# Loading and turning the memory rows tile by tile behind their own norm vector, with the other norm vectors, the x rows and the angle tables placed later

## The chip, the cores and the metric

The kernel runs on one core of one Trainium2 chip. The metric is the device time of one launch in microseconds. A launch has an execution span (from the first to the last instruction of the core) and about 2 us around it.

## What is computed

A two block transformer layer with 256 tokens (two tiles of 128 rows) of width 1024, in float32, each block with a memory of 256 rows. The change touches only what opens the first block: the keys and values of the memory branch, and the norm of the tokens.

```python
def rms_norm(x, g):
    xf = x.astype(jnp.float32)
    y = xf * lax.rsqrt(jnp.mean(xf * xf, axis=-1, keepdims=True) + EPS)
    return (y * g.astype(jnp.float32)).astype(x.dtype)
...
        h = rms_norm(x, g_norm[layer])
        proj = h @ w_in[layer]
...
        kv_m = (rms_norm(mem, g_mem[layer]) @ w_mem_kv[layer]).reshape(b, m_len, 2, M_HEADS, M_HEAD_DIM)
        k_m = rms_norm(kv_m[:, :, 0], g_kn_m[layer])
        v_m = kv_m[:, :, 1]
```

After that come three attention branches with gates, a second block (differential attention, a gated linear recurrence, cross attention), and a mixture of 32 experts of which each token takes two. The cosine and sine tables of the positions are needed when the queries and keys of the first block are rotated.

## The kernel before, in words

Each engine has its own program, written by hand in the order in which it runs; semaphores join them. There is no scheduler, so the order of the code is the order of the work.

The opening, engine by engine. SyncE issues the loads: all 256 memory rows in one transfer (1 MB, into R1v), the first weight block "mk" (columns 0 to 511 of w_mem_kv: row blocks 0 and 1, row blocks 2 and 3, then row blocks 4 to 7), the token rows x (1 MB, into X3), the second weight block "mv" (2 MB), then "cq" and "small". The weight blocks turn through three slots of a ring, so "small" waits until the product of "mk" is done, and "qi" until that of "mv" is. ScalarE issues nine small loads of norm vectors into the 55 rows of GR (g_norm first, g_mem second) and the positions.

TensorE turns (transposes) the 55 rows of norm vectors at once, then the memory rows (four groups of four 128 by 128 transposes, into four banks of PSUM), runs `project("mk", ...)` (two token tiles, eight row blocks i each, 16 matmuls), turns the x rows, and runs `project_blocks("mv", ...)`: seven half-size products m0 to m6 that take the place of eight. m2 and m3 take sums of weights (S_a, S_b), m4 and m6 take the changed blocks w21 and w12; GpSimd makes these four in `weight_sums` (16 additions, each of 128 by 256), and counts them in w_sums. m2 to m5 take sums of the turned rows, which VectorE makes in `row_sums`. m4 is the first product that writes to the accumulator that "mk" used, so it waits until ScalarE has emptied it.

In the profile each float32 matmul or transpose of 128 rows stands as two records.

VectorE copies the turned norm vectors to GC, multiplies the turned memory rows by g_mem while moving them out of PSUM (`drain_rows`), computes the reciprocal root for the memory rows (12 small instructions in `rsqrt`), waits for the squares of x, scales x (`norm_rows`), makes the row sums of memory, makes the arguments of the angle tables (16 small instructions), drains the turned x rows, and combines the products of "mv" (`combine`). The tokens' squares are taken by ScalarE only after VectorE has given the scale of the memory rows (mem_scaled). ScalarE's sine (L1507) waits for the arguments (trig_arg), and its emptying of "mk" (`drain_mem`, L1512) is behind the sine in its program.

After "mv" the order on TensorE is "cq", "small", "qi" and so on; before "cq" it waits until the x rows are drained.

Of the kernel before, what the change touches and what calls it, by code (L numbers as in the profile page):

```python
# [20 lines left out]
ALU = mybir.AluOpType  # L21
ACT = mybir.ActivationFunctionType
AX_X = mybir.AxisListType.X

P = 128
D = 1024
# [26 lines left out]
GC_NORM, GC_MEM, GC_MIX, GC_CROSS, GC_MEM2, GC_CQ, GC_CKV, GC_GATEB, GC_FFN, GC_N = 0, 8, 16, 24, 32, 40, 43, 45, 47, 55  # L53
# [3 lines left out]
def two_block_layer(nc, A, out):  # L57
    ctx = ExitStack()
    with ctx:
# [3 lines left out]
        def sem(name):  # L63
            return ctx.enter_context(nc.semaphore(name))
# [149 lines left out]
        mem_landed = sem("mem_landed")  # L214
# [231 lines left out]
        for t in range(TT):  # L446
# [5 lines left out]
            ("g_norm", GC_NORM, 8), ("g_mem", GC_MEM, 8), ("norm_mix_2", GC_MIX, 8), ("norm_cross_2", GC_CROSS, 8),  # L452
# [41 lines left out]
        def _(pe):  # L494
# [8 lines left out]
            def aux(b, key):  # L503
                n = aux_uses[b]
                aux_uses[b] += 1
                aux_no[key] = (b, n)
                if n:
                    pe.wait_ge(aux_free[b], n)
                return AUX[b], aux_full[b]
# [229 lines left out]
            pe.wait_ge(consts_ready, 1)  # L739
            pe.wait_ge(gains_landed, 16 * len(gains))  # L740
            bank, full = aux(3, "gains")
            nc.tensor.transpose(bank[:, 0:GC_N], GR[:, :], ident[0:GC_N, 0:GC_N]).then_inc(full, 1)
            pe.wait_ge(mem_landed, 16)
            for t in range(TT):
                for g in range(2):
                    turn(2 * t + g, ("mem", t, g))
            project("mk", R2T)
            turn_rows("x0", 0)
            project_blocks("mv", R2T, T_x, mem_sums)
# [441 lines left out]
        def _(sp):  # L1191
            sp.dma_start(R1v, rows(A["mem"])).then_inc(mem_landed, 16)
            for c, (name, width, parts) in enumerate(chunks):
                if slot_before[c]:
                    wait_full(sp, last_job[slot_before[c]])
                for first, src in parts:
                    k, n = src.shape[1], src.shape[2]
                    dst = slot_of(name)[:, 0:k, first:first + n]
                    if c == 0:
                        for i in range(2):  # L1200
                            sp.dma_start(dst[:, 2 * i:2 * i + 2, :], src[:, 2 * i:2 * i + 2, :]).then_inc(first_landed[i], 16)
                        dst, src = dst[:, 4:KD, :], src[:, 4:KD, :]
                    sp.dma_start(dst, src).then_inc(slot_landed[slot_no[c]], 16)
# [75 lines left out]
        def _(pool):  # L1279
# [8 lines left out]
            g.memset(ident[:, :], 0.0)  # L1288
# [7 lines left out]
            for j in range(16):  # L1296
# [3 lines left out]
            g.affine_select(out=ident[:, :], in_=ident[:, :], compare_op=ALU.not_equal, fill=1.0, base=0,  # L1300
                            pattern=[[-1, P]], channel_multiplier=1)
# [126 lines left out]
        def _(act):  # L1428
# [69 lines left out]
            for dst, src in gains:  # L1498
                act.dma_start(dst, src).then_inc(gains_landed, 16)
# [3 lines left out]
            square_rows(0, R1v, R3v, [(mem_landed, 16)])  # L1503
            act.wait_ge(mem_scaled, 1)
            square_rows(1, X3, ZTv, [(x_landed, 16)])
            act.wait_ge(trig_arg, 2)
            a_.activation(trig[:, 128:192], trig[:, 64:128], ACT.Sin).then_inc(trig_ready, 1)  # L1507
# [14 lines left out]
            last.then_inc(mv_scaled, 1)  # L1522
            drain("cq", by_token(PJ3, PJ_CQ, 384))
# [231 lines left out]
        def _(dve):  # L1755
# [198 lines left out]
            bank = wait_full(dve, "gains")  # L1954
            v.tensor_copy(GC[:, :], bank[:, 0:GC_N]).then_inc(free_sem("gains"), 1)
            wait_drained(dve, "gains")
            drain_rows("mem", R2T, GC_MEM)
# [3 lines left out]
            norm_rows(1, X3, ZTv, 2)  # L1961
            row_sums(T_x, quarters(R2T), mem_sums)

# [18 lines left out]
            drain_rows("x0", XT3, GC_NORM)  # L1982
            combine("mv", by_rows(R1v, 512))
# [459 lines left out]
```

## Time and profile before

| | |
|---|---|
| median of three runs | 1104.6 us (1104.5 to 1105.12) |
| the profiled execution's own time | 1104.28 us |
| its span | 1102.5 us |
| busy in the span | TensorE 921.5 us, VectorE 405.2 us, GpSimd 244.4 us, ScalarE 166.9 us |
| first matmul record | 9.17 us after the span's start |
| start of "cq" | 42.85 us |
| moved between 720 and 1080 us | 427 GB/s all the time |

The shares are means over stages with different limits. The last 420 us stream the experts' weights, and the DMA engines are the ones that are full there; before that TensorE is busy nearly all the time, except in the opening, where it has nothing to do for 9 us.

### The profile page before, as it was taken

Reading aid. Unit: us, or ns where it says so; the run is one execution under the profiler, and the core shown is the slowest. Engines: PE = TensorE matmul, PEld = TensorE weight load, DVE = VectorE, ACT = ScalarE, POOL = GpSimd, SP = SyncE. Lnnn points to the kernel's source line nnn. Section 1 sums busy time; section 2 is a strip of 40 time slices with the busy share of each in tenths; the row PEclk is TensorE's granted clock in tenths of the full one; section 3 lists DMA queues with packets and bytes.
Section 4 is the critical chain, followed back from the end, with each engine's and each line's share of the span. In section 5 each row is a group of like instructions: output and inputs, shape, how many; then the busy total and the mean of one; then the engine's idle time right before and its main releaser. Section 6 shows DMA issues by size and latency. Waiting matters only on the chain.

```text
span 1102.5 us, 12492 instructions
## 1 busy us (share of the span) xinstructions
PE 921.5 (84%) x5006; PEld 569.7 (52%) x5006; DVE 405.2 (37%) x994; ACT 166.9 (15%) x372; POOL 244.4 (22%) x366
## 2 busy tenths in 40 slices
PE   6999999999999999999999998757465566473757
PEld 3774487889999878864445653222222122131312
DVE  4736836663223746868445433010101001010101
ACT  2113223441001013013302230000000000000000
POOL 4442143044654958930000000000000000000000
PEclk9999999999999999999999999878878878687879
DMA  7645342232445344524419649999999999999996
GB/s 286 168 146 191 121 153 78 77 130 100 157 168 207 105 171 169 201 87 153 153 68 346 252 173 428 427 429 427 428 428 427 427 428 427 428 429 427 427 416 272
DMA packets 64328, 290.38 MB, mean 263 GB/s; under 512 B 9031, under 2 KB 11918, under 8 KB 51726
## 3 DMA queue, kind: packets, MB, share of 16 engines
q1 hardware_dynamic: 57840, 205.13, 48.6%
q10 hardware_dynamic: 6430, 84.44, 18.1%
q8 instruction: 41, 0.67, 0.3%
q14 instruction: 17, 0.14, 0.0%
HBM read 288.51 MB, written 1.05 MB: 263 GB/s over the span
## 4 chain that ended last, share of the span: by engine, by line
PE 62%; DMA 26%; DVE 6%; issue 2%; another core or an unknown queue 2%; ACT 2%; ACTq 0%; SPq 0%; DVEq 0%
DMA ring<-in_w_e_up_dram 12%; PE ACC L535 10%; PE ACC L691 10%; DMA BIG<-in_w_e_up_dram 9%; PE ACC L550 9%; PE PAIR L1086 8%; PE ACC L688 7%; PE ACC L574 5%; DMA PJ<-in_w_e_up_dram 4%; PE ACC L977 3%; PE PAIR L585 2%; PE PAIR L1117 2%; PE PAIR L662 1%; PE PAIR L639 1%
## 5 line engine op out<-in xcount | busy, mean ns | idle before, releaser
L1337 POOL TENSOR_TENSOR ring<-ring 128x256 f32<-128x256 f32 x272 | 205.3, 785 | 167.3 <-PE ACC L688 75.5
L1086 PE MATMUL PAIR<-ring,R 128*32 128x512 f32 x400 | 130.4, 708 | 41.2 <-DMA BIG<-in_w_e_up_dram 20.8
L550 PE MATMUL ACC<-BIG,ring 128*128 128x256 f32 (+1 forms) x464 | 103.8, 381 | 0.6 <-DVE R L1921 0.6
L550 PEld LDWEIGHTS ACC<-BIG,ring 128*128 128x128 f32 (+1 forms) x464 | 85.4, 187 | 15.5 <-issue 3.1
L2378 DVE SCALAR_TENSOR_TENSOR GB<-GB,PAIR 128x512 f32<-128x512 f32 x8 | 5.5, 688 | 231.8 <-ACT GB L1728 231.8
L1086 PE MATMUL PAIR<-BIG,R 128*32 128x512 f32 x176 | 62.8, 727 | 22.1 <-DMA PJ<-in_w_e_up_dram 22.1
L1086 PE MATMUL PAIR<-R 128*32 128x512 f32 x176 | 59.7, 695 | 25.0 <-DMA ring<-in_w_e_up_dram 12.5
L1117 PE MATMUL PAIR<-ring,BIG 128*32 128x512 f32 x160 | 64.5, 747 | 18.0 <-DMA R<-in_w_e_down_dram 12.4
L535 PE MATMUL ACC<-ring,BIG 128*128 128x512 f32 (+2 forms) x192 | 78.1, 559 | 0.5 <-DVE R L2214 0.5
L1086 PE MATMUL PAIR<-SQE,R 128*32 128x512 f32 x112 | 61.4, 711 | 17.0 <-DMA ring<-in_w_e_up_dram 10.7
L1086 PEld LDWEIGHTS PAIR<-ring,R 128*32 128x32 f32 x400 | 30.9, 128 | 73.2 <-issue 73.2
L691 PE MATMUL ACC<-ring 128*128 128x256 f32 x288 | 64.9, 381 | 1.9 <-ACT R L1512 1.0
L535 PE MATMUL ACC<-ring,R 128*128 128x512 f32 (+1 forms) x136 | 59.1, 584 | 0.7 <-DVE R L2007 0.4
L691 PEld LDWEIGHTS ACC<-ring 128*128 128x128 f32 x288 | 54.3, 190 | 10.4 <-issue 1.8
L1117 PE MATMUL PAIR<-PJ,BIG 128*32 128x512 f32 x128 | 46.7, 746 | 14.4 <-DMA ring<-in_w_e_down_dram 14.4
L2380 DVE SCALAR_TENSOR_TENSOR GB<-GB,PAIR 128x512 f32<-128x512 f32 x8 | 8.4, 1052 | 131.8 <-PE PAIR L1086 131.8
L574 PE MATMUL ACC<-ring,BIG 128*128 128x512 f32 x128 | 55.8, 592 | 0.0
L1086 PE MATMUL PAIR<-PJ,R 128*32 128x512 f32 x160 | 50.8, 698 | 5.7 <-DMA ring<-in_w_e_up_dram 5.0
L535 PEld LDWEIGHTS ACC<-ring,BIG 128*128 128x128 f32 x192 | 35.6, 190 | 35.2 <-issue 27.0
L688 PE MATMUL ACC<-ring 128*128 128x128 f32 x384 | 45.1, 276 | 0.0
L688 PEld LDWEIGHTS ACC<-ring 128*128 128x128 f32 x384 | 44.1, 192 | 0.7 <-issue 0.5
L691 PE MATMUL ACC<-ring,R 128*128 128x256 f32 x184 | 40.9, 379 | 0.0
(346 smaller groups left out, 1402.5 us busy)
## 6 DMA issues: line engine op xcount, KB each, us to landing
ring<-in_w_in_dram SPq DMA_DIRECT2D x20, 2048.0 KB, 7.9
ring<-in_w_e_gate_dram SPq DMA_DIRECT2D x8, 2048.0 KB, 40.1
ring<-in_w_e_up_dram SPq DMA_DIRECT2D x6, 2048.0 KB, 41.1
ring<-in_w_e_gate_dram ACTq DMA_DIRECT2D x6, 2048.0 KB, 26.5
ring<-in_w_e_down_dram SPq DMA_DIRECT2D x5, 2048.0 KB, 39.1
ring<-in_w_e_up_dram ACTq DMA_DIRECT2D x5, 2048.0 KB, 20.9
ring<-in_w_ckv_dram SPq DMA_DIRECT2D x4, 2048.0 KB, 8.0
BIG<-in_w_e_down_dram SPq DMA_DIRECT2D x4, 2048.0 KB, 22.9
```

Source lines behind the costliest of these rows:

```text
L535: mm = nc.tensor.matmul(bank[:, t * 512:t * 512 + width], lhs[:, i, t * P:(t + 1) * P], w[:, i, a:a + width], start=(i == 0), stop=(i == k ...
L550: mm = nc.tensor.matmul(bank[0:m, j * S:(j + 1) * S], w[:, i, a + j * P:a + j * P + m], rhs[:, i, :], start=(i == 0), stop=(i == k - 1))
L574: mm = nc.tensor.matmul(bank[:, c:c + 512], lhs[:, i, t * P:(t + 1) * P], w[:, i, :], start=(i == order[0]), stop=(i == order[-1]))
L585: mm = nc.tensor.transpose(bank[0:src.shape[1], j * P:(j + 1) * P], src, ident[:, :])
L639: mm = nc.tensor.transpose(bank[:, (j * heads + i) * P:(j * heads + i + 1) * P], e[:, i, j * P:(j + 1) * P], ident[:, :])
L662: mm = nc.tensor.matmul(bank[:, d * 256:(d + 1) * 256], value(j, h, d), p[:, j * 256:(j + 1) * 256], start=first, stop=last)
L688: mm = nc.tensor.matmul(bank[:, j * P:(j + 1) * P], left[:, k, j * P:(j + 1) * P], right[:, k, :], start=(k == 0), stop=(k == 3))
L691: mm = nc.tensor.matmul(bank, right[:, k, :], left[:, k, :], start=(k == 0), stop=(k == 3))
L977: mm = nc.tensor.matmul(ACC[t][:, h * 512:(h + 1) * 512], XT3[:, i, t * P:(t + 1) * P], slot_of(f"wco{h}")[:, i, :], start=False, stop=Fal ...
L1086: mm = nc.tensor.matmul(bank[r, :], M_xt[:, k, r], w[e][:, k, :], start=(k == 0), stop=(k == KD - 1))
L1117: mm = nc.tensor.matmul(AUX[2 + h][r, :], M_hidt[:, k, r], w[e][:, k, h * 512:(h + 1) * 512], start=(k == 0), stop=(k == 3))
L1337: ins = g.tensor_tensor(out[:, k, :], a[:, k, :], b[:, k, :], op)
```

## The change

The load of the memory rows is split into its two tiles; the second is issued behind row blocks 0 to 3 of "mk". The norm vector g_mem moves to the front of GR and of ScalarE's loads and gets a semaphore of its own; it is turned alone, and the other vectors are turned later, inside "mk", together with the second tile of memory rows. GpSimd finishes the identity matrix first and signals it. The turning of x moves from ahead of "mv" to behind its fourth product. On VectorE the row sums of memory move ahead of the norm of x, the angle arguments behind the combination of "mv"; on ScalarE the squares of x move ahead of the wait for mem_scaled, and the sine behind the emptying of "mk" and "mv".

```diff
-GC_NORM, GC_MEM, GC_MIX, ... = 0, 8, 16, ...
+GC_MEM, GC_NORM, GC_MIX, ... = 0, 8, 16, ...
...
 TensorE
-            pe.wait_ge(consts_ready, 1)
-            pe.wait_ge(gains_landed, 16 * len(gains))
-            bank, full = aux(3, "gains")
-            nc.tensor.transpose(bank[:, 0:GC_N], GR[:, :], ident[0:GC_N, 0:GC_N]).then_inc(full, 1)
-            pe.wait_ge(mem_landed, 16)
-            for t in range(TT):
+            pe.wait_ge(ident_ready, 1)
+            pe.wait_ge(mem_gain_landed, 16)
+            nc.tensor.transpose(ACC[1][:, 0:8], GR[0:8, :], ident[0:8, 0:8]).then_inc(mem_gain_turned, 1)
+
+            def turn_mem(t):
+                pe.wait_ge(mem_landed[t], 16)
                 for g in range(2):
                     turn(2 * t + g, ("mem", t, g))
-            project("mk", R2T)
-            turn_rows("x0", 0)
-            project_blocks("mv", R2T, T_x, mem_sums)
+            def turn_rest(done, total):
+                if done == 4:
+                    turn_mem(1)
+                    pe.wait_ge(gains_landed, 16 * (len(gains) - 1))
+                    nc.tensor.transpose(ACC[1][:, 512:512 + GC_N], GR[:, :], ident[0:GC_N, 0:GC_N]).then_inc(gains_turned, 1)
+
+            turn_mem(0)
+            pe.wait_ge(consts_ready, 1)
+            project("mk", R2T, after=turn_rest)
+            pe.wait_ge(gains_ready, 2)
+            project_blocks("mv", R2T, T_x, mem_sums, after=lambda done: turn_rows("x0", 0) if done == 16 else None)
...
 SyncE
-            sp.dma_start(R1v, rows(A["mem"])).then_inc(mem_landed, 16)
+            sp.dma_start(R1v[:, 0, :], A["mem"][0, 0:P, :]).then_inc(mem_landed[0], 16)
...
                             sp.dma_start(dst[:, 2 * i:2 * i + 2, :], src[:, 2 * i:2 * i + 2, :]).then_inc(first_landed[i], 16)
+                        sp.dma_start(R1v[:, 1, :], A["mem"][0, P:2 * P, :]).then_inc(mem_landed[1], 16)
...
 GpSimd
-            g.memset(ident[:, :], 0.0)
+            link(g.memset(ident[:, :], 0.0))
+            g.affine_select(out=ident[:, :], in_=ident[:, :], compare_op=ALU.not_equal, fill=1.0, base=0,
+                            pattern=[[-1, P]], channel_multiplier=1).then_inc(ident_ready, 1)
...
 ScalarE
-            for dst, src in gains:
+            act.dma_start(*gains[0]).then_inc(mem_gain_landed, 16)
+            for dst, src in gains[1:]:
                 act.dma_start(dst, src).then_inc(gains_landed, 16)
...
-            square_rows(0, R1v, R3v, [(mem_landed, 16)])
+            act.wait_ge(mem_landed[0], 16)
+            a_.activation(R3v[:, 0, :], R1v[:, 0, :], ACT.Square, scale=D ** -0.5, accum_out=SMALL[:, 64:65])
+            square_rows(0, R1v, R3v, [(mem_landed[1], 16)], [1])
+            square_rows(1, X3, ZTv, [(x_landed, 16)], col=66)
             act.wait_ge(mem_scaled, 1)
-            square_rows(1, X3, ZTv, [(x_landed, 16)])
-            act.wait_ge(trig_arg, 2)
-            a_.activation(trig[:, 128:192], trig[:, 64:128], ACT.Sin).then_inc(trig_ready, 1)
...
             last.then_inc(mv_scaled, 1)
+            act.wait_ge(trig_arg, 2)
+            a_.activation(trig[:, 128:192], trig[:, 64:128], ACT.Sin).then_inc(trig_ready, 1)
             drain("cq", by_token(PJ3, PJ_CQ, 384))
...
 VectorE
-            bank = wait_full(dve, "gains")
-            v.tensor_copy(GC[:, :], bank[:, 0:GC_N]).then_inc(free_sem("gains"), 1)
-            wait_drained(dve, "gains")
-            drain_rows("mem", R2T, GC_MEM)
+            dve.wait_ge(mem_gain_turned, 1)
+            v.tensor_copy(GC[:, 0:8], ACC[1][:, 0:8]).then_inc(gains_ready, 1)
+            dve.wait_ge(gains_ready, 1)
+            drain_rows("mem", R2T, GC_MEM, [0])
+            drain_rows("mem", R2T, GC_MEM, [1])
+            dve.wait_ge(gains_turned, 1)
+            v.tensor_copy(GC[:, 8:GC_N], ACC[1][:, 520:512 + GC_N]).then_inc(gains_ready, 1)
+            dve.wait_ge(gains_ready, 2)
             dve.wait_ge(rows_squared, 1)
             rsqrt(2, SMALL[:, 64:66])
             v.tensor_copy(SMALL[:, 74:76], RS[:, 0:2]).then_inc(mem_scaled, 1)
-            norm_rows(1, X3, ZTv, 2)
+            for t in range(TT):
+                for g in range(2):
+                    wait_drained(dve, ("mem", t, g))
             row_sums(T_x, quarters(R2T), mem_sums)
+            norm_rows(1, X3, ZTv, 2, col=66)
+            drain_rows("x0", XT3, GC_NORM)
+            combine("mv", by_rows(R1v, 512))
...
-            drain_rows("x0", XT3, GC_NORM)
-            combine("mv", by_rows(R1v, 512))
             dve.wait_ge(small_landed, small_total)
```

TensorE's program at its start, before (PAIR and ACC are banks of PSUM, SQE holds the norm vectors, R the memory rows and later their turned form, BIG the x rows and later their turned form, ring the weights; one row for each instruction, xN for N alike):

```order
L742 MATMUL PAIR<-ident,SQE 128x55
L585 MATMUL PAIR<-ident,R 128x128 x16
L535 MATMUL ACC<-ring,R 128x512 x16
L585 MATMUL PAIR<-ident,BIG 128x128 x16
L691 MATMUL ACC<-ring,R 128x256 x8
L691 MATMUL ACC<-ring 128x256 x16
L691 MATMUL ACC<-ring,R 128x256 x4
L535 MATMUL ACC<-ring,BIG 128x384 x16
```

The same place in the changed kernel (its line numbers are a few higher):

```order
L745 MATMUL ACC<-ident,SQE 128x8
L589 MATMUL PAIR<-ident,R 128x128 x8
L539 MATMUL ACC<-ring,R 128x512 x4
L589 MATMUL PAIR<-ident,R 128x128 x8
L756 MATMUL ACC<-ident,SQE 128x55
L539 MATMUL ACC<-ring,R 128x512 x12
L695 MATMUL ACC<-ring,R 128x256 x8
L695 MATMUL ACC<-ring 128x256 x8
L589 MATMUL PAIR<-ident,BIG 128x128 x16
L695 MATMUL ACC<-ring 128x256 x8
L695 MATMUL ACC<-ring,R 128x256 x4
L539 MATMUL ACC<-ring,BIG 128x384 x16
```

Half of the memory's transposes moved into "mk" behind its fourth matmul, with the turning of all vectors behind them; the x transposes moved from ahead of "mv" to between its fourth and fifth products.

ScalarE's program behind its loads, before (the table load at L1507 and the activation with PJ are the sine):

```order
L1442 ACT_TABLE_LOAD
L1442 ACTIVATE BIG,SMALL<-R 128x1024 x2
L1442 ACTIVATE BIG,SMALL<-BIG 128x1024 x2
L1507 ACT_TABLE_LOAD
L1507 ACTIVATE PJ<-PJ 128x64
L1512 ACTIVATE R<-ACC,SMALL 128x512 x2
L1452 ACTIVATE SQE<-R 128x1024
L1521 ACTIVATE R<-R,SMALL 128x512 x2
L1458 ACTIVATE PJ<-ACC 128x384 x2
```

The same place in the changed kernel:

```order
L1519 ACT_TABLE_LOAD
L1519 ACTIVATE BIG,SMALL<-R 128x1024
L1456 ACTIVATE BIG,SMALL<-R 128x1024
L1456 ACTIVATE BIG,SMALL<-BIG 128x1024 x2
L1527 ACTIVATE R<-ACC,SMALL 128x512 x2
L1466 ACTIVATE SQE<-R 128x1024
L1536 ACTIVATE R<-R,SMALL 128x512 x2
L1539 ACT_TABLE_LOAD
L1539 ACTIVATE PJ<-PJ 128x64
L1472 ACTIVATE PJ<-ACC 128x384 x2
```

The sine and its table load moved from ahead of the emptying of "mk" (R<-ACC) to behind the scaling of "mv", just ahead of the emptying of "cq".

## Rows read from the trace of the kernel before

**Rows 1.** The page: busy time, share of the span, instructions.

```profile
PE 921.5 (84%) x5006; PEld 569.7 (52%) x5006; DVE 405.2 (37%) x994; ACT 166.9 (15%) x372; POOL 244.4 (22%) x366
```

**Rows 2.** The chain that ended last, 0 to 120 us: start, us, what.

```profile
4.21 4.82 DMA SQE<-in_norm_ffn_dram
...
36.36 1.16 ACT R L1512 x2
```

**Rows 3.** Timeline of TensorE: start, us, what, idle before with releaser.

```profile
9.42 3.67 PE L585 MATMUL PAIR<-ident,R 128*128 128x128 f32 x16
12.89 15.02 PE L535 MATMUL ACC<-ring,R 128*128 128x512 f32 x32
27.75 1.91 PE L585 MATMUL PAIR<-ident,BIG 128*128 128x128 f32 x16
...
37.56 3.72 PE L691 MATMUL ACC<-ring 128*128 128x256 f32 x16 [1.00 <-ACT R L1512]
...
42.85 20.16 PE L535 MATMUL ACC<-ring,BIG 128*128 128x384 f32 x64
```

**Rows 4.** DMA issues, 0 to 60 us: size, median us to landing; then SyncE's first issue.

```profile
R<-in_mem_dram SPq DMA_DIRECT2D x1, 1024.0 KB, 5.0
ring<-in_w_mem_kv_dram SPq DMA_DIRECT2D x2, 512.0 KB, 6.7
ring<-in_w_mem_kv_dram SPq DMA_DIRECT2D x1, 1024.0 KB, 9.8
...
0.82 0.44 SPq L1192 DMA_DIRECT2D R<-in_mem_dram  x1
2.39 0.65 SPq L1203 DMA_DIRECT2D ring<-in_w_mem_kv_dram  x1
```

**Rows 5.** DMA queue of ScalarE, 0 to 2 and 2.5 to 3 us (packets); all queues, 4.5 to 5.

```profile
q10 hardware_dynamic: 12, 0.00, 0.6%
q10 hardware_dynamic: 4, 0.00, 0.8%
4.50:5.00 0.50, 0.00 (x0) 0.00 (x0) 0.00 (x0) 0.00 (x0) 0.23 (x2) 1.00 1.02 401
```

**Rows 6.** Timeline of GpSimd.

```profile
4.64 0.15 POOL L1312 MEMSET MASKS<- 64x64 f32 x1
20.30 10.93 POOL L1337 TENSOR_TENSOR ring<-ring 128x256 f32<-128x256 f32 x12 [15.51 <-DMA ring<-in_w_mem_kv_dram]
33.26 2.77 POOL L1337 TENSOR_TENSOR ring<-ring 128x256 f32<-128x256 f32 x4 [2.03 <-PE ACC L691]
```

**Rows 7.** Matmuls of "mk", 12.8 to 13.3 and 15.6 to 16.2 us: busy, mean ns.

```profile
L535 PE MATMUL ACC<-ring,R 128*128 128x512 f32 x1 | 1.1, 1061 | 0.0
L535 PE MATMUL ACC<-ring,R 128*128 128x512 f32 x3 | 1.5, 592 | 0.0
```

**Rows 8.** Timeline of VectorE.

```profile
22.43 2.31 DVE L1793 TENSOR_SCALAR BIG<-BIG,RS 128x1024 f32<-128x1024 f32 x2
24.67 1.21 DVE L1935 TENSOR_TENSOR ring<-R 128x512 f32<-128x512 f32 x1
...
35.42 0.65 DVE L1979 TENSOR_SCALAR PJ<-PJ 128x32 f32<-128x32 f32 x1
36.10 2.48 DVE L1806 TENSOR_TENSOR BIG<-PAIR,GC 128x512 f32<-128x512 f32 x4
...
39.74 0.42 DVE L1917 TENSOR_TENSOR R<-ACC,R 128x256 f32<-128x256 f32 x1
...
65.91 0.17 DVE L1767 TENSOR_SCALAR NW<-SMALL 128x4 f32<-128x4 f32 x1 [11.38 <-ACT SQE L1531]
```

**Rows 9.** Timeline of ScalarE.

```profile
53.37 0.87 ACT L1458 ACTIVATE PJ<-ACC 128x384 f32<-128x384 f32 x2 [8.53 <-PE ACC L535]
```

**Rows 10.** SyncE's waits, 560 to 700 us; then the window of the expert stage.

```profile
SPq L1245 <- PE ACC L977: 29.8, 2, 20.6
720.00:1080.00 360.00, 220.89 (x1480) 81.88 (x1484) 29.74 (x64) 13.04 (x24) 0.00 (x0) 0.79 1.01 427
```

More of the change, by code:

```diff
@@ L51 @@
 PJ_QA, PJ_KA, PJ_VA, PJ_QI, PJ_KI, PJ_WI, PJ_CKV, PJ_KR, PJ_CQ, PJ_QM, PJ_W = 0, 512, 1024, 1536, 2048, 2112, 2120, 2376, 2408, 2792, 3304
-GC_NORM, GC_MEM, GC_MIX, GC_CROSS, GC_MEM2, GC_CQ, GC_CKV, GC_GATEB, GC_FFN, GC_N = 0, 8, 16, 24, 32, 40, 43, 45, 47, 55
+GC_MEM, GC_NORM, GC_MIX, GC_CROSS, GC_MEM2, GC_CQ, GC_CKV, GC_GATEB, GC_FFN, GC_N = 0, 8, 16, 24, 32, 40, 43, 45, 47, 55
 GB_A, GB_B, GB_M, GB_DA, GB_DAO, GB_GLAO, GB_X, GB_ROUTE, GB_LAM, GB_N = 0, 128, 320, 576, 704, 832, 960, 1472, 1508, 1764
@@ L213, in two_block_layer @@
         x_landed = sem("x_landed")
-        mem_landed = sem("mem_landed")
+        mem_landed = [sem(f"mem_landed{t}") for t in range(TT)]
+        mem_gain_landed = sem("mem_gain_landed")
+        mem_gain_turned = sem("mem_gain_turned")
+        gains_turned = sem("gains_turned")
+        ident_ready = sem("ident_ready")
         mem2_landed = sem("mem2_landed")
@@ L451, in two_block_layer @@
         gains = [(GR[r:r + n, :], A[name][0].rearrange("(k p) -> k p", p=P)) for name, r, n in (
-            ("g_norm", GC_NORM, 8), ("g_mem", GC_MEM, 8), ("norm_mix_2", GC_MIX, 8), ("norm_cross_2", GC_CROSS, 8),
+            ("g_mem", GC_MEM, 8), ("g_norm", GC_NORM, 8), ("norm_mix_2", GC_MIX, 8), ("norm_cross_2", GC_CROSS, 8),
             ("norm_mem_2", GC_MEM2, 8), ("g_cq", GC_CQ, 3), ("g_ckv", GC_CKV, 2),
@@ L1299, in _ @@
             g.tensor_copy(iota[:, :], iota_i[:, :])
-            g.affine_select(out=ident[:, :], in_=ident[:, :], compare_op=ALU.not_equal, fill=1.0, base=0,
-                            pattern=[[-1, P]], channel_multiplier=1)
             g.affine_select(out=causal[:, 128:256], in_=causal[:, 128:256], compare_op=ALU.is_ge, fill=NEG, base=0,
```

## The prediction

> **What bounds the kernel now.** I read the shares of busy time first [rows 1]: TensorE is busy for 84% of the span, no other engine for half of it. Then the chain that ended last [rows 2]. It opens with the last norm vector, whose load is issued at 4.21 and takes 4.82 us to land, and later it runs over ScalarE's emptying of "mk" at 36.36. The timeline of TensorE [rows 3] shows both as idle time: its first transposes of memory rows start only at 9.42, and ahead of 37.56 stands a wait of 1.00 us for ScalarE. Between these, and up to the start of "cq" at 42.85, it has no other gap. So two things bound the opening: what TensorE waits for before its first work, and that one wait. The expert stage at the end is bound otherwise: from 720 to 1080 us 427 GB/s are moved without a break, with TensorE busy 221 of 360 us [rows 10]. A gain in the opening reaches the end only if that stream starts earlier too. Its first loads are issued when TensorE has finished something (SyncE waits 29.8 us for the matmuls of L977 in two waits) [rows 10], so it should move along.
>
> **The start.** The changed kernel needs for its first memory transposes: the first memory tile, g_mem turned, and the identity. The 1 MB of memory rows is issued at 0.82 and lands 5.0 us later, at 5.8 [rows 4]; half of it is 0.52 MB less, which at 401 GB/s is 1.3 us [rows 5]. So the first tile lands at about 4.5. g_mem is now the first load on ScalarE's queue. In the trace the first one is g_norm, with eight rows: 12 packets of that queue ran before 2 us and 4 between 2.5 and 3 [rows 5], which is eight rows and eight counts, so I take 3.0 for it. GpSimd's last constant ends at 4.79 [rows 6]; the identity is now its first. So the memory transposes start at 4.5 in place of 9.42: **4.9 us**. As bounds I take 4.2 us (the half tile saves only half of the 1.3 us) and 5.5 us: GpSimd's constants at 4.79, a copy (0.2 us) and a drain (0.69 us) let no first matmul start before 5.7, and the forecast has 6.3.
>
> **"mk".** 16 transposes take 3.5 us (9.42 to 12.89), so the first eight end at 6.2. VectorE may not begin before its constants (4.8), then drains a group in 0.69 us at most (four took 2.48 [rows 8]), so the first matmul starts at about 6.3. Row blocks 0 to 3 of "mk" lie in two loads of 512 KB. With the first memory tile ahead they are the second and third half megabyte, at about 5.8 and 7.1; in time. Here the clock matters. The granted clock in the profile's rows is 1.00 for all of the opening, but the records speak otherwise: the first matmul of "mk" has 1061 ns, those after 15.6 have 592 ns [rows 7]. The transposes too run at 0.22 us each at 9.42 and at 0.12 us at 27.75 [rows 3]. So until about 15.4 (between the two rows), 6.0 us after its first transpose, the engine ran at 1.2 GHz, then at 2.4. I let the slow stretch keep its 6.0 us: 4.5 to 10.5. Then "mk" has done 4.2 us of slow work by 10.5, which is 2.1 us at full speed; four matmuls are 3.4 us at full speed (a quarter of 15.02 less the 1.3 lost between 12.89 and 15.4), so they end at 11.8. The second memory tile landed at about 8.5; eight transposes (1.0 us) and the turned vectors (0.1) end at 12.9. The last half of "mk" weights lands at 2.39 + 9.8 = 12.2 [rows 4]; no wait. The other 12 matmuls take 10.3 us: "mk" ends at 23.2, against 27.75. Of the 4.9 us 4.6 are still there; the gain work and handing over cost 0.3.
>
> **"mv".** GpSimd starts on the sums at 20.30, when the weights land, and the bytes ahead of them stay the same [rows 6]. They are 12 additions in 10.93 us and 4 in 2.77: 23.9, 27.6, 31.2 and 34.1 are the ends of the four sums at the rate of before, if it no longer waits 2.03 us for TensorE in between. TensorE now reaches m0 at 23.2, each product takes 1.8 us (two in 3.72 [rows 3]): m2 at 26.8, m3 at 28.6, the x transposes 30.4 to 32.3, m4 at 32.3, m5 at 34.1, m6 at 35.9, end 37.7. Each lies behind its sum, by 2.9, 1.0, 1.1 and 1.8 us. The x transposes, which stood ahead of "mv", cover GpSimd's third sum. The wait of 1.00 us goes, since ScalarE empties "mk" at 23.3 with no sine ahead: **1.0 us**. By differences: the seven products and the x transposes took 43.0 - 27.75 = 15.2 us, less 1.0 is 14.2, and 23.2 + 14.2 = 37.4. I take 37.4, a gain of **5.6 us** at the start of "cq".
>
> **VectorE.** The x rows must be scaled by 30.4. Memory is drained at 13.6, then a root of 12 small instructions (2.4 us), row sums (4.6 us at most, from four of 1.1 to 1.2 [rows 8]), another root, and the scaling (2.31 us for two tiles). Beside GpSimd's additions a small instruction takes 0.65 us, otherwise 0.17 [rows 8]. That gives 26 us as I expect it, and with every instruction slow 30.4 for the first tile: no wait, or one of some tenths. The drains of x (2.5 us) end at 33; the combination's third part (three instructions of 0.42 us [rows 8]) follows m5 and frees the bank for "cq" at 37.2. Cover: 0.2 us only, so what is late here next is this bank.
>
> **What moved behind.** The angle arguments took 6.9 us (29.2 to 36.1 [rows 8]) and now start at 37.8. They are beside four additions of GpSimd, as before; 7 us, 45. The sine is needed by ScalarE before it empties "cq", which is full at 37.4 + 10.1 = 47.5 (it was at 53.37 [rows 9]). Then the memory keys' norm (7 us) to 52, and the next thing on VectorE, the latents' root, is due at 65.91 - 5.6 = 60.3 [rows 8]; it idled 11.38 us ahead of it before. So these moves cost nothing. The extra load instruction on SyncE (0.44 us) is covered by the full DMA queue.
>
> **Sum.** 4.9 + 1.0 - 0.3 = 5.6 us off an execution of 1104.28 (span 1102.5): 1098.7. The median is 0.3 above this execution, so 1099.0.
>
> **A rule against the change.** The loads of the opening follow each other at 401 GB/s with 512 KB pieces among them [rows 5], so one more piece costs nothing that I can see. The Trainium skill, page SBUF — State Buffer, section on the DMA setup-cost knee, says that each transfer pays about 2 us that don't scale with bytes and that one should coalesce into the largest transfer; by that the last half of "mk" would land 2 us later, and the sum would be about 3.5 in place of 5.6. The trace disagrees as far as it shows queued loads.
>
> **The rivals.**
> - *The slow clock lasts longer or shorter.* Work is now thinner at the start, with a drain to wait for. If the clock rises when the fourth matmul is done instead of at 10.5, these end at 6.3 + 6.8 = 13.1 and not 11.8: 1.3 us lost, and the eight transposes half a us more, 1100.8. If it rises as long after the first matmul as before (15.4 - 12.9 = 2.5, at 8.8), the four end at 11.0, but the weights at 12.2 stop the gain at 0.7: 1098.3. The Trainium skill (TensorE: Matmul & The Clock Gate, what's actually happening) calls the number of slow matmuls at a start run-variable.
> - *A load lands later than worked out.* Cutting the memory load moves later ones by a us or two: "mk" waits at its fifth matmul from 12.9 to 14.2, and the sums of "mv" shift too. 1.3 to 2.1 us lost: 1100.3 to 1101.1. For it: the fifth matmul comes only 0.7 us behind its weights now. Against it: no byte is added ahead of "mk".
> - *The gain does not reach the end.* The expert stream is full for 400 us; if its start hung on a load and not on TensorE, the end would stay: 1104.6. Against it stand SyncE's waits [rows 10].
> - *Slower: VectorE's queue.* Angle arguments and the keys' norm stand ahead of the latents' root in one queue. If both ran three times as long beside GpSimd (0.65 for 0.17 us on each small instruction and more), 14 us would be 42, ending at 80 instead of 60.3. It decides from 28 us on: 22.5 us is the cover, and 5.6 more eat the gain. In the trace the arguments already ran half of their time beside GpSimd and took 6.9 us, so I see no such thing; 1105 to 1110 if it came.
>
> **How the numbers follow.** The forecast (1098.4 to 1100.0) has 0.57, the clock earlier 0.10, clock later 0.12, loads later 0.11, no gain at the end 0.06, slower 0.04. The range 1097.9 to 1101.4 holds the first four. Within 0.2% (2.2 us, about what a measurement of this kernel can tell from no change) is only a gain lost almost wholly. Faster 0.91, same 0.05, slower 0.04.
>
> **What would show it.** First memory transpose at 4.5; records of 1061 ns until about 10.5; no idle TensorE ahead of the fifth matmul of "mk", of m3, m4 and m6; ScalarE's emptying of "mk" right behind its end; "cq" from 37.3. From there on every start should be 5.6 earlier up to the last store. It is wrong if the first transposes start after 6, if GpSimd's sums end after 36, or if the stream between 680 and 1080 does not move.

## The result

The changed kernel takes 1098.42 us (1098.32 to 1098.58, four runs) against 1104.55 us (1103.96 to 1105.12, four runs) of the kernel before: ratio 0.9945, 95% interval 0.9933 to 0.9957. It is 6.1 us faster; 5.6 was forecast. The profiled execution took 1098.47 us, with a span of 1096.6.

The page after, busy time by engine, hardly differs from before [rows 1]:

```profile
PE 922.8 (84%) x5007; PEld 569.3 (52%) x5007; DVE 403.1 (37%) x995; ACT 167.2 (15%) x372; POOL 243.1 (22%) x366
```

Timeline of TensorE of the changed kernel (start, us, line, what; in brackets the idle time ahead with its releaser), which answers to [rows 3]:

```profile
3.15 0.24 PE L745 MATMUL ACC<-ident,SQE 8*128 8x8 f32 x1 [3.15 <-DMA SQE<-in_g_mem_dram]
4.66 1.97 PE L589 MATMUL PAIR<-ident,R 128*128 128x128 f32 x8 [1.27 <-DMA R<-in_mem_dram]
6.68 4.68 PE L539 MATMUL ACC<-ring,R 128*128 128x512 f32 x8
11.20 1.04 PE L589 MATMUL PAIR<-ident,R 128*128 128x128 f32 x8
...
12.51 10.54 PE L539 MATMUL ACC<-ring,R 128*128 128x512 f32 x24
22.89 3.62 PE L695 MATMUL ACC<-ring,R 128*128 128x256 f32 x16
...
29.80 1.91 PE L589 MATMUL PAIR<-ident,BIG 128*128 128x128 f32 x16
31.54 3.62 PE L695 MATMUL ACC<-ring 128*128 128x256 f32 x16
...
36.73 20.16 PE L539 MATMUL ACC<-ring,BIG 128*128 128x384 f32 x64
```

The memory transposes start at 4.66 in place of 9.42, the end of "mk" is at 22.89 in place of 27.75, and "cq" starts at 36.73 in place of 42.85. So 4.86 us are there at the end of "mk", and the rest of the 6.12 us, 1.26, comes inside "mv", where the wait for ScalarE ahead of m4 is gone.

The chain that ended last, in the changed kernel's first 60 us (start, us, what). The vectors' load, VectorE and ScalarE, which it ran over before [rows 2], are no longer in it:

```profile
0.82 3.80 DMA R<-in_mem_dram
...
4.66 1.97 PE PAIR L589 x8
...
12.51 10.54 PE ACC L539 x24
...
31.71 5.18 PE ACC L695 x24
```

Timelines of GpSimd, VectorE and ScalarE in the changed kernel, which answer to [rows 6, 8, 9]:

```profile
20.52 12.24 POOL L1351 TENSOR_TENSOR ring<-ring 128x256 f32<-128x256 f32 x16 [15.50 <-DMA ring<-in_w_mem_kv_dram]
```

```profile
15.82 0.69 DVE L1952 TENSOR_TENSOR ring<-R 128x512 f32<-128x512 f32 x1
...
21.29 2.31 DVE L1810 TENSOR_SCALAR BIG<-BIG,RS 128x1024 f32<-128x1024 f32 x2
30.43 2.48 DVE L1823 TENSOR_TENSOR BIG<-PAIR,GC 128x512 f32<-128x512 f32 x4 [6.83 <-PE PAIR L589]
...
36.00 0.42 DVE L1938 TENSOR_TENSOR R<-ACC,R 128x256 f32<-128x256 f32 x1
...
37.38 0.97 DVE L1993 CAST NW<-pos_i 128x2 f32<-128x2 int32 x1
...
59.79 0.17 DVE L1784 TENSOR_SCALAR NW<-SMALL 128x4 f32<-128x4 f32 x1 [7.87 <-ACT SQE L1548]
```

```profile
23.15 1.27 ACT L1527 ACTIVATE R<-ACC,SMALL 128x512 f32<-128x512 f32 x2 [5.99 <-PE ACC L539]
...
44.68 0.26 ACT L1539 ACTIVATE PJ<-PJ 128x64 f32<-128x64 f32 x1 [4.66 <-DVE PJ L2005]
47.25 0.87 ACT L1472 ACTIVATE PJ<-ACC 128x384 f32<-128x384 f32 x2 [2.31 <-PE ACC L539]
```

The 16 additions run through in 12.24 us without a wait. The row sums of memory run at 15.82, before GpSimd starts, at 0.69 us each; before they stood beside its additions at 1.21. ScalarE empties "mk" at 23.15, as soon as it is full. The sine is at 44.68 and "cq" is there to be emptied at 47.25, after 2.31 us of idle time, so the cover of the sine is 2.3 us. The latents' root still finds VectorE idle for 7.87 us.

The gain reaches the end. SyncE's loads of w_co, before at 572.24, and the late first-round loads of the experts, before at 658.54, have moved by 6.14 and 6.15 us (SyncE's timeline, changed kernel):

```profile
566.10 0.99 SPq L1217 DMA_DIRECT2D ring<-in_w_co_dram  x2
...
652.39 3.33 SPq L1259 DMA_DIRECT2D BIG<-in_w_e_down_dram  x2
```

The stream behind moves 426 GB/s from 720 to 1080 us, 427 before [rows 10]. The store of the result is issued at 1091.27, before at 1097.51; the spans differ by 5.9 us, since the end behind that issue was 0.3 us longer in this profile.

### The profile page after: what moved, and what is told of

It reads as the page before. It is cut to its first block, busy times and chain, and to the rows that moved or that the text cites. A ratio compares the mean times of both kernels' runs of the same rounds, so it can differ in the third digit from the quotient of the medians.

```text
span 1096.6 us, 12500 instructions
## 1 busy us (share of the span) xinstructions
PE 922.8 (84%) x5007; PEld 569.3 (52%) x5007; DVE 403.1 (37%) x995; ACT 167.2 (15%) x372; POOL 243.1 (22%) x366
## 4 chain that ended last, share of the span: by engine, by line
PE 62%; DMA 31%; DVE 5%; ACT 1%; issue 1%; SPq 0%; DVEq 0%; ACTq 0%
DMA ring<-in_w_e_up_dram 12%; PE ACC L539 12%; PE ACC L695 10%; DMA PJ<-in_w_e_up_dram 9%; DMA BIG<-in_w_e_up_dram 9%; PE ACC L554 9%; PE PAIR L1099 7%; PE ACC L692 7%; PE ACC L578 5%; PE ACC L990 3%; PE PAIR L589 2%; PE PAIR L666 1%; PE PAIR L643 1%; PE PAIR L724 1%; PE PAIR L1130 1%
## 5 line engine op out<-in xcount | busy, mean ns | idle before, releaser
L1130 PE MATMUL PAIR<-PJ,BIG 128*32 128x512 f32 x128 | 47.5, 759 | 13.3 <-DMA ring<-in_w_e_down_dram 13.3
```

The costliest lines, as they stand in the source:

```text
L1130: mm = nc.tensor.matmul(AUX[2 + h][r, :], M_hidt[:, k, r], w[e][:, k, h * 512:(h + 1) * 512], start=(k == 0), stop=(k == 3))
```

## The experiments

Single executions of one kernel differed by up to 3.6 us within one group, more than some of the effects, and the medians of the kernel before lie between 1103.99 and 1104.55 us from group to group. So beside each median stands the start of "cq" in the profiled execution: 42.85 before, 36.73 changed. What comes behind it is the same work in all kernels. The start of "cq" too holds a part that is no work of the edit: in the eight profiles without dummy matmuls the first four matmuls of "mk" took between 4.24 and 5.77 us, by when the records get fast.

**One part alone: sine and angle arguments.**

```diff
 kernel before; ScalarE
-            act.wait_ge(trig_arg, 2)
-            a_.activation(trig[:, 128:192], trig[:, 64:128], ACT.Sin).then_inc(trig_ready, 1)
...
             last.then_inc(mv_scaled, 1)
+            act.wait_ge(trig_arg, 2)
+            a_.activation(trig[:, 128:192], trig[:, 64:128], ACT.Sin).then_inc(trig_ready, 1)
 VectorE: drain_rows("x0", ...) and combine("mv", ...) ahead of the angle arguments
```

> The kernel before, with one part of the change alone: the angle arguments on VectorE behind the combination of mv, and the sine on ScalarE behind the scaling of mv. Theory (the gain is an earlier start plus the wait of m4 that goes): m4 no longer waits, 1.0 us of idle time and 0.26 us of refilling go, so 1.2 to 1.3 us off, about 1103.3, with TensorE's first transposes still near 9.4. Rival (the wait only changes hands, because something else than the sine is late, or the other moves are needed for it): 1104.5, with another releaser ahead of m4 or of cq.

Measured: 1102.66 us (before 1104.07; ratio 0.9982, 0.9973 to 0.9992), 1.4 us off. TensorE's timeline:

```profile
9.20 3.67 PE L585 MATMUL PAIR<-ident,R 128*128 128x128 f32 x16
12.67 14.44 PE L535 MATMUL ACC<-ring,R 128*128 128x512 f32 x32
...
32.14 7.07 PE L691 MATMUL ACC<-ring 128*128 128x256 f32 x32
...
40.77 19.56 PE L535 MATMUL ACC<-ring,BIG 128*128 128x384 f32 x62
```

"cq" is 2.08 us earlier than before, of which 0.22 is the start, 0.59 "mk" with fewer slow records (14.44 for 15.02), and the rest, 1.27, the wait: the four products from 32.14 on now run without one. The theory holds, and the wait needs none of the other moves to go. The interval of the times (0.9 to 3.0 us off) fits this and shuts out the rival's nothing.

**The memory in one load.**

```diff
 changed kernel; SyncE
-            sp.dma_start(R1v[:, 0, :], A["mem"][0, 0:P, :]).then_inc(mem_landed[0], 16)
+            sp.dma_start(R1v, rows(A["mem"])).then_inc(mem_landed[0], 16)
...
-                        sp.dma_start(R1v[:, 1, :], A["mem"][0, P:2 * P, :]).then_inc(mem_landed[1], 16)
 TensorE and ScalarE: the waits for the second tile are for this load
```

> The changed kernel with the memory rows in one load of 1 MB at the front, both tiles still turned where the change puts them. Theory (start of TensorE set by the landing of the first memory tile): first transposes at 5.8 to 5.9 in place of 4.66, everything 1.2 us later, about 1099.6. Rival (the fifth matmul of mk waits for its weights at 12.35 whatever comes ahead, so that the split is hidden): 1098.4 to 1098.8.

Measured: 1100.31 us (before 1104.07; ratio 0.9962, 0.9948 to 0.9976).

```profile
5.99 1.97 PE L589 MATMUL PAIR<-ident,R 128*128 128x128 f32 x8 [3.39 <-DMA R<-in_mem_dram]
8.01 4.30 PE L539 MATMUL ACC<-ring,R 128*128 128x512 f32 x8
...
13.30 10.57 PE L539 MATMUL ACC<-ring,R 128*128 128x512 f32 x24
```

The start is 1.33 us later, "cq" at 37.55 only 0.82 later, since the four matmuls took 4.30 instead of 4.68 us and the changed kernel had arrived just at its weights. The profiled execution was the fastest of five (1098.81). By the medians the split is worth 1.9 us against the changed kernel's 1098.42 and 1.0 against its 1099.35 of the last group: about 1 us, and not known more closely. The rival, in which nothing is lost, falls.

**All vectors turned ahead of memory.**

```diff
 changed kernel; TensorE, ahead of the memory rows
-            nc.tensor.transpose(ACC[1][:, 0:8], GR[0:8, :], ident[0:8, 0:8]).then_inc(mem_gain_turned, 1)
+            pe.wait_ge(gains_landed, 16 * (len(gains) - 1))
+            nc.tensor.transpose(ACC[1][:, 0:GC_N], GR[:, :], ident[0:GC_N, 0:GC_N]).then_inc(mem_gain_turned, 1)
 TensorE: no second turning inside "mk"; VectorE: all 55 columns copied at once
```

> The changed kernel, but TensorE waits for all nine norm vectors and turns them at once ahead of the memory rows. Theory: first transposes near 9.3, 4.6 us later than in the changed kernel; only the wait of m4 stays removed, so 1103.0 to 1103.4. Rival (the vectors, now loaded beside a smaller first transfer, land much earlier, since the queue of ScalarE was held up by the 1 MB load): start at 5 to 7 and 1099 to 1101.

Measured: 1102.24 us (1101.4 to 1104.23; ratio 0.998, 0.997 to 0.9989), "cq" at 41.58, 4.85 us later than changed.

```profile
8.92 0.32 PE L746 MATMUL ACC<-ident,SQE 55*128 55x55 f32 x1 [8.92 <-DMA SQE<-in_norm_ffn_dram]
...
11.19 5.55 PE L539 MATMUL ACC<-ring,R 128*128 128x512 f32 x8
```

The memory transposes start at 9.17, 4.51 us later, and the slow records cost 0.87 us more in this execution. It took 1103.57, which is 5.1 more than the profiled execution of the changed kernel; the medians are 3.8 us apart, and 2.9 with the changed kernel's 1099.35. So the vector of its own is the largest part of the gain, 3 to 4 us of time and 4.5 of start. The rival falls: a smaller first transfer does not free ScalarE's queue, the last vector still lands at 8.9.

**The x transposes ahead of "mv".**

```diff
 changed kernel; TensorE
-            project_blocks("mv", R2T, T_x, mem_sums, after=lambda done: turn_rows("x0", 0) if done == 16 else None)
+            turn_rows("x0", 0)
+            project_blocks("mv", R2T, T_x, mem_sums)
```

> The changed kernel with the x transposes ahead of mv again, as before. The prediction had them cover GpSimd's third sum, which it put at 31.2. The trace of the changed kernel has all four sums done at 32.76, so the third near 30, and m4 at 31.54. Theory now: m2 at 28.2, m3 at 30.0, m4 at 31.6 all lie behind their sums, and x is scaled by 23.6; the order is worth nothing or 0.1 to 0.7 us for the wait of the second x tile: 1098.4 to 1099.1. Rival (the cover is needed): a wait at m4 of 1 us or more, 1099.4 and above.

Measured: 1098.8 us (ratio 0.9953, 0.9936 to 0.997), "cq" at 36.71. This move is worth nothing: the cover that the prediction gave the x transposes is not needed. The profile shows no wait at m2 to m6, but one ahead of the fifth matmul of "mk", where TensorE came earlier than its weights this time:

```profile
12.50 10.54 PE L539 MATMUL ACC<-ring,R 128*128 128x512 f32 x24 [0.45 <-DMA ring<-in_w_mem_kv_dram]
```

**Sine and arguments back.** The edit of the first experiment undone in the changed kernel.

```diff
 changed kernel; ScalarE, ahead of drain_mem
+            act.wait_ge(trig_arg, 2)
+            a_.activation(trig[:, 128:192], trig[:, 64:128], ACT.Sin).then_inc(trig_ready, 1)
 VectorE: the angle arguments ahead of drain_rows("x0", ...) and combine("mv", ...)
```

> The changed kernel with the angle arguments on VectorE ahead of the x drains again and the sine ahead of the emptying of mk. Theory: the arguments start at 23.6 beside GpSimd's additions, where a small instruction takes 0.65 us, and end at 31 to 34.5; the sine, the emptying of mk and the x drains follow, so m4 waits 1 to 4 us and cq for the x drains: 1100.5 to 1102.5. Rival (with the earlier start there is room for them): 1098.4 to 1098.9.

Measured: 1105.1 us (1103.4 to 1107.04; ratio 1.0005, 0.9995 to 1.0014): the whole gain is gone, more than I expected (1102.5 at most). TensorE's timeline, and its windows (busy of PE, weight loads, VectorE, ScalarE, GpSimd; granted clock, DMA share, GB/s) of this kernel:

```profile
30.98 1.91 PE L589 MATMUL PAIR<-ident,BIG 128*128 128x128 f32 x16
37.14 6.03 PE L695 MATMUL ACC<-ring 128*128 128x256 f32 x16 [4.25 <-ACT R L1529]
```

```profile
33.00:37.00 4.00, 0.00 (x0) 0.00 (x0) 3.78 (x11) 2.61 (x4) 0.00 (x0) 0.75 0.14 39
37.00:40.00 3.00, 2.86 (x7) 2.33 (x8) 1.34 (x4) 1.14 (x2) 0.00 (x0) 0.50 0.71 115
40.00:42.00 2.00, 2.00 (x7) 1.62 (x6) 0.00 (x0) 0.00 (x0) 0.00 (x0) 0.54 0.23 52
42.00:45.00 3.00, 3.00 (x15) 2.59 (x14) 1.25 (x4) 0.00 (x0) 0.00 (x0) 1.00 0.07 12
```

The wait at m4 is 4.25 us, just above the 4 that I expected at most. VectorE and ScalarE show why (arguments; sine; emptying of "mk"):

```profile
27.12 0.69 DVE L1990 CAST NW<-pos_i 128x2 f32<-128x2 int32 x1
```

```profile
35.68 0.26 ACT L1524 ACTIVATE PJ<-PJ 128x64 f32<-128x64 f32 x1
35.84 1.25 ACT L1529 ACTIVATE R<-ACC,SMALL 128x512 f32<-128x512 f32 x2
```

The arguments start at 27.12 and not at the 23.6 of the forecast, because the root of the x rows ahead of them began 1.3 us later than in the first profile of the changed kernel (19.66 for 18.36) and so fell beside the additions (0.65 us for a small instruction). GpSimd starts these when the weights land, at 20.57, and that did not move. "mk" is emptied from 35.84 on, before from 36.26 in the same view: TensorE started 4.54 us earlier, and 0.42 of it are left at m4. So the two gains do not simply add up. The sine moved alone is worth 1.3 us; without it the earlier start comes back as a longer wait.

During the wait the granted clock fell, at 35.0, to 0.50 of full, and it stayed there until 41.8, so m4 and m5 took 6.03 us and not 3.62. The wait alone is 4.25, the fallen clock 2.4 more. This execution was the slowest of ten (1107.04); the fastest was at 1103.4, and I take it, without a profile of it, that the clock did not fall or not as long there.

**Dummy matmuls, and the weights of "mk" in more parts.** The first kernel adds eight matmuls of the identity by itself, into a bank that "mk" overwrites; the second loads the last half of the weights in two parts; the third does both.

```diff
 changed kernel; TensorE (first and third)
             pe.wait_ge(ident_ready, 1)
+            for i in range(8):
+                nc.tensor.matmul(ACC[0][:, 0:128], ident[:, :], ident[:, :], start=True, stop=True)
 SyncE (second and third; TensorE waits for half_landed at i = 4 and for the chunk at i = 6)
-                        dst, src = dst[:, 4:KD, :], src[:, 4:KD, :]
+                        sp.dma_start(dst[:, 4:6, :], src[:, 4:6, :]).then_inc(half_landed, 16)
+                        dst, src = dst[:, 6:KD, :], src[:, 6:KD, :]
```

> The changed kernel with eight extra matmuls of the identity by itself, into a bank that mk later overwrites, as soon as the identity is there (near 1.5 us): TensorE is busy before the memory rows land. Theory: the clock rises earlier (records of 421 ns for the memory transposes turn to 273 ns), up to 1.5 us of slow work saved ahead of the fifth matmul of mk; but that matmul's weights land at 12.35 and it now comes at 12.43, so the time stays, 1098.3 to 1098.5, with a new wait for the load. Rival (the start is bound by TensorE's own work, not by the load): 1097 to 1097.5.

> The changed kernel with the last half of the mk weights in two loads of 512 KB, each with its own wait. Theory: nothing, TensorE arrives at its fifth matmul when all has landed: 1098.3 to 1098.6. Rival (each further transfer costs some 2 us that do not scale with bytes): mv lands later, GpSimd starts later than 20.5 and the time rises by 0.5 us or more.

> Both: the eight extra matmuls at the start and the last half of the mk weights in two loads. Theory: the load no longer stops the gain of the earlier clock; four matmuls end at 9.8 to 10, the fifth comes at 11 behind its half load, mk ends 1 to 1.4 us earlier, and the sums of GpSimd (last at 32.8) still lie ahead of m6: 1097.0 to 1097.6. Rival (the sums of GpSimd, which start at 20.5 whatever TensorE does, take it back): waits at m3 or m4 and 1098.2 to 1098.5.

Measured: 1097.96, 1097.76 and 1098.01 us (ratios 0.9951, 0.9948, 0.9945, each with an interval of 0.0016 or 0.0017 to either side; 6.0, 6.2 and 6.0 us off the 1103.99 of the kernel before in this group, as the changed kernel is 6.1 off in its own), "cq" at 36.82, 36.50 and 35.72. The three timelines of TensorE in this order:

```profile
1.59 3.78 PE L745 MATMUL ACC<-ident 128*128 128x128 f32 x16 [1.59 <-POOL ident L1305]
...
5.51 1.97 PE L589 MATMUL PAIR<-ident,R 128*128 128x128 f32 x8
7.52 3.67 PE L539 MATMUL ACC<-ring,R 128*128 128x512 f32 x8
...
12.61 10.54 PE L539 MATMUL ACC<-ring,R 128*128 128x512 f32 x24 [0.35 <-DMA ring<-in_w_mem_kv_dram]
```

```profile
12.26 10.57 PE L542 MATMUL ACC<-ring,R 128*128 128x512 f32 x24
```

```profile
5.26 1.09 PE L592 MATMUL PAIR<-ident,R 128*128 128x128 f32 x8
6.82 3.67 PE L542 MATMUL ACC<-ring,R 128*128 128x512 f32 x8 [0.46 <-DVE R L1829]
```

In the first the dummies did not help the memory transposes (1.97 us, slow as ever, and 0.85 late behind the dummies), but the four matmuls ran at full speed in 3.67; then the weights stopped it, 0.35 us of wait, and "cq" is where it was. That is what the theory said. The more parts alone had "cq" 0.2 us earlier, which is what the four matmuls took less (4.51 for 4.68), and did not delay the weights of "mv" (GpSimd starts at 20.43), so the further transfer cost nothing that shows. Both together bring "cq" forward by 1.0 us. In the medians that is not seen in this group (1098.01 for an expected 1097.0 to 1097.6); the group below repeats it.

**The last group**: the changed kernel again; both edits again; both edits with a halved first tile; and the row sums put back.

```diff
 with both edits; SyncE (each half is turned when it has landed; VectorE's wait for consts_ready behind the first drains)
-            sp.dma_start(R1v[:, 0, :], A["mem"][0, 0:P, :]).then_inc(mem_landed[0], 16)
+            sp.dma_start(R1v[:, 0, 0:512], A["mem"][0, 0:P, 0:512]).then_inc(mem_half, 16)
+            sp.dma_start(R1v[:, 0, 512:D], A["mem"][0, 0:P, 512:D]).then_inc(mem_landed[0], 16)
```

```diff
 changed kernel; ScalarE
-            square_rows(1, X3, ZTv, [(x_landed, 16)], col=66)
             act.wait_ge(mem_scaled, 1)
+            square_rows(1, X3, ZTv, [(x_landed, 16)], col=66)
 VectorE: norm_rows(1, X3, ZTv, 2, col=66) ahead of row_sums(T_x, ...)
```

> The changed kernel again, as the reference of this group. 1098.0 to 1098.6, 6 us below the kernel before, with cq at 36.7 or up to a microsecond around it by when the clock rises.

> The kernel with dummy matmuls and parts again, in one group with the changed kernel. Theory: cq at 35.7 where the dummies raise the clock before the memory transposes, 36.5 where they do not; so 0.3 to 1.0 us below the changed kernel, 1097.4 to 1098. Rival (the dummies do nothing): equal to it.

> The kernel with the dummy matmuls and the weights of mk in more parts, and besides the first memory tile in two loads of 256 KB, each half turned when it has landed, and VectorE's wait for GpSimd's constants behind the first drains. Theory (the start is still set by the landing of the first rows): first group turned from 4.2 to 4.4 in place of 4.7 to 5.3, first matmul at 6.1 to 6.4, cq at 35.2 to 35.5, about 1097.0. Rival (GpSimd's sums, fixed by the landing of the mv weights at 20.5, now bind): waits at m3 or m4 that leave cq at 35.6 or later.

> The changed kernel with the squares of x on ScalarE behind the wait for the scale of the memory rows again, and on VectorE the norm of x ahead of the row sums of memory, as before. Theory: the row sums start at 22 to 23 and are done by 27.6, each just ahead of the product that takes it (m2 at 26.3 needs the first); GpSimd's sums run beside them at the slower rate of before (second at 27.6 against m3 at 28.1). So nothing to 0.5 us: 1098.2 to 1098.8. Rival (this move is a part of the gain): waits at m2 or m3 of 1 us or more.

Measured, against 1104.03 us of the kernel before: changed again 1099.35 (1097.92 to 1099.68; ratio 0.9949, 0.9936 to 0.9962), both edits 1097.59 (1097.27 to 1100.43; 0.9943, 0.9931 to 0.9955), halved first tile 1097.88 (1097.41 to 1100.1; 0.9944, 0.9931 to 0.9957), row sums back 1098.67 (1098.18 to 1098.99; 0.9948, 0.9935 to 0.9961). "cq" at 37.50, 35.56, 37.43 and 37.41.

The changed kernel's own times fall into two sets, 1097.92 and 1098.11, and 1099.35 to 1099.68. The profile is of the second. Its start, at 4.76, is 0.1 us later than in the first result, and the rest of the difference is in the slow records:

```profile
6.77 5.49 PE L539 MATMUL ACC<-ring,R 128*128 128x512 f32 x8
...
13.26 10.57 PE L539 MATMUL ACC<-ring,R 128*128 128x512 f32 x24
```

Four matmuls took 5.49 us there and 4.68 above. With both edits they take 3.67 in both profiles, and the memory transposes 1.09. That version has the lowest median of its group and "cq" 1.2 us ahead of the first profile of the changed kernel and 1.9 ahead of the second. Its interval overlaps that of the changed kernel, so that it is faster is shown by the profiles, not by the times.

The halved first tile went wrong in the profiled execution (1099.06 us, one of the slower two of five): the transposes end early, but the first weights of "mk" land 1.8 us after them, and those of "mv" at 22.0, not 20.4. TensorE and GpSimd of this kernel:

```profile
5.51 1.22 PE L593 MATMUL PAIR<-ident,R 128*128 128x128 f32 x8
8.52 3.67 PE L543 MATMUL ACC<-ring,R 128*128 128x512 f32 x8 [1.79 <-DMA ring<-in_w_mem_kv_dram]
```

```profile
22.01 12.05 POOL L1361 TENSOR_TENSOR ring<-ring 128x256 f32<-128x256 f32 x16 [16.97 <-DMA ring<-in_w_mem_kv_dram]
```

Between 4.5 and 6 us the DMA engines moved 215 GB/s there, against 382 in the kernel with both edits. Whether the smaller pieces or something else delayed all loads by 1.5 us stays open; it was one execution. Neither the theory's gain nor the rival's wait at m3 or m4 came. The gain could not have come at the start in any case: the dummy matmuls and the vector keep TensorE busy until 5.5 us (5.1 and 5.3 in the two profiles with both edits), and the halves, issued at 0.82 and 1.26, landed by about 4.2. The theory left that out.

With the row sums back GpSimd's additions take longer, and m3 waits for the second sum (TensorE and GpSimd):

```profile
28.65 1.99 PE L695 MATMUL ACC<-ring 128*128 128x256 f32 x8 [0.26 <-POOL ring L1351]
```

```profile
20.39 13.95 POOL L1351 TENSOR_TENSOR ring<-ring 128x256 f32<-128x256 f32 x16 [15.35 <-DMA ring<-in_w_mem_kv_dram]
```

13.95 against 12.24 us. The idle time is 0.26 us, but from the start of m2 to that of the x transposes it is 3.97 us, and 3.46 in the changed kernel: this move is worth half a microsecond at "cq", and what it holds in reserve. The rival's wait of 1 us or more did not come.

One part was not undone by itself: the identity signalled ahead of the other constants. GpSimd's last constant ends at 5.02 in the changed kernel; with the vector's turning (0.25 us) behind it the memory transposes would start at about 5.3 in place of 4.66. So 0.6 us of the start is an estimate for this part, and no run shows it.

## Why the prediction was right

The mechanism came as forecast, and the forecast of the time was 0.6 us too high. The terms of the sum were 4.9 for the start, 0.3 lost in "mk" and 1.0 in "mv", 5.6 in all; measured are 4.76, 0.10 gained, and 1.26, 6.12 in all. The errors in "mk" and "mv" went the same way. The forecast also added 0.3 us for a median above the profiled execution, and that did not come: the two are 1098.42 and 1098.47.

- **The start.** Forecast 4.5, measured 4.66: 4.76 us earlier for the 4.9 of the sum. g_mem was turned at 3.15, as its landing at 3.0 said. Undone singly, the turning of the vector by itself cost 2.9 to 3.8 us by the medians (4.5 at the start, 4.85 at "cq" with its slower records), and the split of the rows 1.0 to 1.9 (1.33 at the start, 0.82 at "cq").
- **"mk".** The forecast let the slow clock last 6.0 us from the first transpose. That was read a little long already: in the kernel before, the record that starts at 14.60 takes 867 ns and the one at 15.30 593, so the records got fast at about 15.1 and not 15.4. Here the stretch was shorter still: four matmuls took 4.68 us and not 5.5. The fifth began at 12.51 and not 12.9, with its weights landed at 2.75 + 9.6 = 12.35, so that the load was just about to bind. This was the rival of the shorter clock, in part; its time of 1098.3 is nearer to 1098.42 than the forecast of 1099.0. That the profiled execution had the shorter stretch is luck of when the clock rose, and so is this part of the gain. In the second profile the four took as long as forecast (5.49 us, fifth matmul at 13.26), and that execution took 1099.35. The slow records are 0.8 of the 0.9 us by which the two profiled executions differ; that they also part the other executions is likely and not shown. The Trainium skill (TensorE: Matmul & The Clock Gate, what's actually happening) calls the number of slow matmuls run-variable, and these two profiles of one kernel agree with it.
- **"mv".** The wait was put at 1.0 us, its idle time. It was worth 1.26: from the start of the second pair of products to that of the third it was 4.61 us, and without the wait 3.45, which is 1.16; the other 0.1 lies in the third pair. This is the term that was put too small.
- **GpSimd's sums.** They were put at the rate of before, and the x transposes were to cover the third. That step was wrong in size and needless: 16 additions took 12.24 us, not 13.7, because the row sums on VectorE no longer run beside them (13.95 us with them back), and with the x transposes ahead again no product waits.
- **What moved behind.** The arguments took 7.3 us (37.38 to 44.65) for the 7 forecast, the sine came at 44.68 for 45, "cq" was to be emptied at 47.25. The bank for "cq" was free at 36.42, 0.3 us ahead of its use. As said, nothing waits.
- **To the end.** All of SyncE's later loads moved by 6.1 us; the rival in which the stream does not start earlier falls. The slower rival did not come either. Its mechanism, small instructions slowed beside GpSimd, is there (0.65 us and more for 0.17), but where the arguments now stand VectorE still has 7.87 us to spare ahead of the latents' root. It costs time where the arguments stand ahead of the emptying of "mk", as with the sine put back.
- **The rule against the change** in the Trainium skill (SBUF — State Buffer, the DMA setup-cost knee), by which each transfer pays about 2 us, did not bear on the split in two: the last half of the "mk" weights landed at 12.35 for 12.2 before, the "mv" weights at 20.5 for 20.3. Whatever one more load costs by itself, behind others in the queue it showed as 0.2 us at most. The halved first tile, with weights 1.5 us late, may be a case of it; one execution does not show that.

## What to carry to other kernels

Look at what the first instruction of the busiest engine really needs, and give exactly that a load and a semaphore of its own at the front of its queue: here one vector of 4 KB, held back by eight that nobody needed yet, was worth 3 to 4 us, more than the halving of a 1 MB load. A small task that waits in an in-order queue ahead of the emptying of an accumulator makes the accumulator late; put it where the engine idles anyway. Before you bring a start forward, look for the wait behind it that hangs on something else: here it would have eaten nearly all of the gain. And price a wait of the matrix engine by the starts around it and by the clock, not by its idle time alone.

## What the runs showed of the hardware

- One kernel took 1097.9 to 1098.1 us in two executions of a group and 1099.4 to 1099.7 in three. Two of its profiles (1098.47 and 1099.35 us) differ by how many of the first matmuls ran at half speed (4.68 and 5.49 us for four of them), with the waits alike within 0.1 us.
- Eight matmuls of the identity during the initial wait brought the memory transposes to full speed in two of three profiles of kernels with a whole first tile (1.09 us for eight), and in one not (1.97), where the four matmuls behind them ran at full speed.
- In a wait of 4.25 us, behind 28 us of nearly unbroken work, the granted clock fell to 0.50 at 35.0, 2.1 us after the last matmul, and came back at 41.8, though TensorE was busy again from 37.1. So the 4.25 us of wait brought another 2.4 us with them, on two products (one profile).
- VectorE and GpSimd slowed each other: a VectorE addition of 128x512 with both inputs in SBUF took 0.69 us alone and 1.1 to 1.2 beside GpSimd's additions, and 16 of those took 12.24 us without and 13.95 with four such on VectorE. VectorE's four drains out of PSUM took 2.48 us, beside them or not.
- One small load can hold SyncE's queue: in the changed kernel the issue of the load of b_group (2 KB) took 3.84 us (30.98 to 34.82), before 1.20, and the "qi" weights went out at 37.87, 1.1 us after the start of "cq" and not 0.2 as before. GpSimd started on them at 49.28, 11 us before TensorE asked for the sums, so it cost nothing here.
